# The start of the expert stage: expert 0 on unsplit weights, the third tile's weights loaded earlier, three tiles in another order

## The reference, cut to what matters

```python
def moe(h, w_router, router_bias, w_gate_l, w_up_l, w_down_l):   # cut
    scores = jax.nn.sigmoid((t @ w_router).astype(F32))
    ...                                        # best group, then top 2 of its experts
    gate = jnp.einsum('td,edf->tef', t, w_gate_l)
    up = jnp.einsum('td,edf->tef', t, w_up_l)
    act = jax.nn.silu(gate) * up * combine[..., None].astype(gate.dtype)
    return jnp.einsum('tef,efd->td', act, w_down_l).reshape(B, N, D)
```

## Time and profile before

| | us |
|---|---|
| median of 3 runs | 2196.75 (2194.47 to 2199.99) |
| the profiled execution | 2201.26 |
| its span | 2199.5 |
| TensorE busy | 1997.4 (91%) |
| VectorE, ScalarE, GpSimd busy | 1030.8, 849.7, 354.9 |

### The profile page before, as it was taken

The page is one execution under the profiler, slowest core; times in us unless marked ns, Lnnn a source line. Parts: engine busy times, 40 slices in busy tenths (PEclk is TensorE's granted clock), DMA queues, the critical chain, the costliest instruction groups (busy, mean ns, idle before and its releaser), DMA issues. The chain is left out here.

```text
span 2199.5 us, 30789 instructions
## 1 busy us (share of the span) xinstructions
PE 1997.4 (91%) x12535; PEld 1633.4 (74%) x12535; DVE 1030.8 (47%) x1744; ACT 849.7 (39%) x1375; POOL 354.9 (16%) x135
## 2 busy tenths in 40 slices
PE   5989879999999988999949898878999999799994
PEld 4889757678888876676638896557888887567663
DVE  3385246721111246777562852664111123677763
ACT  3443335431111234565434333655111133356553
POOL 2322100012213211000033222000313230200003
PEclk9999889999999998999979998999999999799997
DMA  8212686742221128999542121001212212799864
GB/s 295 72 39 79 211 287 222 259 129 73 70 74 58 44 110 325 318 309 312 194 154 74 39 78 51 1 1 39 86 58 75 70 44 96 289 401 387 302 217 172
DMA packets 163856, 336.31 MB, mean 153 GB/s; under 512 B 10370, under 2 KB 121602, under 8 KB 149252
## 3 DMA queue, kind: packets, MB, share of 16 engines
q1 hardware_dynamic: 151488, 299.63, 39.4%
q0 software_dynamic: 5760, 20.97, 2.5%
q10 hardware_dynamic: 6468, 13.73, 1.7%
HBM read 334.57 MB, written 53.74 MB: 177 GB/s over the span
## 5 line engine op out<-in xcount | busy, mean ns | idle before, releaser
L642 POOL TENSOR_TENSOR wlo<-raw,whi 128x2048 fp32r<-128x2048 f32 x52 | 238.0, 4579 | 1141.1 <-ACT whi L667 1141.1
L1656 DVE TENSOR_TENSOR xw_gu_lo<-xw_gu_raw,xw_gu_hi 128x2048 fp32r<-128x2048 f32 x100 | 228.1, 2284 | 26.6 <-ACT xw_gu_hi L1442 26.6
L184 PE MATMUL psum<-h_hi,whi 128*128 128x320 f32 x896 | 216.6, 323 | 20.4 <-POOL h_lo L177 17.7
L184 PE MATMUL psum<-whi,h_hi 128*128 128x256 f32 x720 | 209.5, 291 | 0.0
L184 PE MATMUL psum<-h_lo,whi 128*128 128x320 f32 x896 | 205.1, 310 | 0.0
L184 PE MATMUL psum<-h_hi,wlo 128*128 128x320 f32 x896 | 204.7, 309 | 0.0
L184 PE MATMUL psum<-wlo,h_hi 128*128 128x256 f32 x720 | 202.9, 282 | 0.0
L184 PE MATMUL psum<-whi,h_lo 128*128 128x256 f32 x720 | 202.8, 282 | 0.0
L814 ACT ACTIVATE sig_m<-psum 128x640 f32<-128x640 f32 x48 | 33.7, 703 | 400.1 <-PE psum L184 400.1
L1442 ACT ACTIVATE xw_gu_hi<-xw_gu_raw 128x2048 fp32r<-128x2048 f32 x100 | 185.4, 1906 | 0.0
L1795 PE MATMUL psum<-xw_d_raw,act_T 128*128 128x512 f32 x400 | 180.0, 593 | 0.9 <-ACT act_T L1468 0.9
(11 more groups left out here) (281 smaller groups left out, 3549.6 us busy)
## 6 DMA issues: line engine op xcount, KB each, us to landing
xw_gu_raw<-w_e_gate SPq DMA_DIRECT2D x50, 1024.0 KB
xw_gu_raw<-w_e_up SPq DMA_DIRECT2D x50, 1024.0 KB
xw_d_raw<-w_e_down SPq DMA_DIRECT2D x50, 1024.0 KB, 9.2
raw<-w_in SPq DMA_DIRECT2D x46, 1024.0 KB, 5.4
wm_rest<-w_mod SPq DMA_DIRECT2D x40, 1024.0 KB, 5.2
y_rows<-y_sel SPq DMA_DIRECT2D x50, 512.0 KB, 9.3
h_sel<-h_rows SPq DMA_DIRECT2D x48, 512.0 KB, 7.6
h_rows<-c_zero ACTq DMA_DIRECT2D x1, 12800.0 KB, 51.6
```

The costliest lines, as they stand in the source:

```text
L184: mm = pe.matmul(dst, st, mv[q], start=start and n == 0, stop=stop and n == 2)
L642: pool.tensor_tensor(wlo[i % 2][:, :, :], raw[i % 2][:, :, :], whi[i % 2][:, :, :].bitcast(F32), ALU.subtract).then_inc(w_lo, 1)
L1656: dve.tensor_tensor(gu_lo[i % 2][:, n, :, :], gu_raw[i % 2][:, n, :, :], gu_hi[i % 2][:, n, :, :].bitcast(F32), ALU.subtract).then_inc(x_l ...
```

## The change

Expert 0's gate/up product is done in fp32 on the weights as loaded (`gu_first`, a buffer of its own at Z + 64K) and on one unsplit copy of its rows (`h_first`), so tile 0 needs no high and low parts, and all counts of these semaphores go down by one. `gu_hi[0]` and `gu_hi[1]` change places. The gate/up load of tile 0 waits for `g_pfree` instead of the last low part of w_out. The load of tile 2's gate/up moves ahead of the wait for the scatters, behind the wait for the index steps; the rows of tiles 1 and 2 are both loaded right after the scatters. VectorE waits for the scatters before the low parts of tile 1. TensorE, ScalarE and VectorE take the first three tiles in an order written out by hand, with TensorE turning tile 2's rows after tile 1's product instead of before it.

```diff
-        gu_hi = [at(f"xw_gu_hi{i}", [P, 2, KD, DE], Z + 80 * K - 16 * K * i, F32R) for i in range(2)]
+        gu_hi = [at(f"xw_gu_hi{i}", [P, 2, KD, DE], Z + 64 * K + 16 * K * i, F32R) for i in range(2)]
+        gu_first = at("xw_gu_first", [P, 2, KD, DE], Z + 64 * K)
+        h_first = at("h_T_first", [P, KD, P], 20 * K)
...                                  # SyncE
-                            if i >= 2:
-                                sp.wait_ge(x_lo[r], i - 1)
-                            load(i, r, gu_raw[i % 2][:, n, :, :], gu_ld[i % 2])
+                            if i >= 3:
+                                sp.wait_ge(x_lo[r], i - 2)
+                            load(i, r, (gu_first if i == 0 else gu_raw[i % 2])[:, n, :, :], gu_ld[i % 2])
...
-                    sp.wait_ge(w_lo, N_STREAM - ahead)
+                    sp.wait_ge(g_pfree, 24)
                     load_gate_up(0)
                     sp.wait_ge(o_full, KD)
                     load_gate_up(1)
                     load_down(0)
+                    sp.wait_ge(w_lo, N_STREAM - ahead)
+                    sp.wait_ge(gu_ld[0], 32)
+                    sp.wait_ge(r_st, IDX_STEPS)
+                    load_gate_up(2)
                     sp.wait_ge(k_s, 16 * 2 * TT)
                     load_h(1)
-                    sp.wait_ge(r_st, IDX_STEPS)
+                    load_h(2)
                     for i in range(N_TILES):
-                        if i + 2 < N_TILES:
+                        if 1 <= i < N_TILES - 2:
                             load_gate_up(i + 2)
                             load_h(i + 2)
...                                  # ScalarE
+                    def h_whole():
+                        act.wait_ge(x_th, 1)
+                        act.activation(h_first[:, :, :].rearrange("p k s -> p (k s)"), flat(1)[:, :], ACT.Copy).then_inc(x_hh, 1)
...
-                    hi(0, "g")
-                    hi(0, "u")
-                    h_high(0)
                     hi(1, "g")
                     hi(1, "u")
+                    h_whole()
                     sigmoid(0)
                     h_high(1)
-                    for i in range(1, N_TILES):
...
+                    keep_act(0)
+                    hi(2, "g")
+                    hi(2, "u")
+                    sigmoid(1)
+                    h_high(2)
+                    for i in range(2, N_TILES):
...                                  # VectorE
-                    lo(0, "g")
-                    h_low(0)
-                    lo(0, "u")
+                    dve.wait_ge(k_s, 16 * 2 * TT)
                     lo(1, "g")
                     lo(1, "u")
                     activated(0)
                     h_low(1)
-                    for i in range(1, N_TILES):
...
+                    lo(2, "g")
+                    lo(2, "u")
+                    activated(1)
+                    h_low(2)
+                    for i in range(2, N_TILES):
...                                  # TensorE
+                    def gate_up_first():
+                        pe.wait_ge(x_hh, 1)
+                        pe.wait_ge(gu_ld[0], 32)
+                        for kc in range(KD):
+                            mm = pe.matmul(psum[:, 0, :], h_first[:, kc, :], gu_first[:, :, kc, :], start=(kc == 0), stop=(kc == KD - 1))
                         mm.then_inc(x_gu, 1)
...
-                    for i in range(N_TILES):
-                        if i >= 1:
-                            turn_act(i - 1)
-                        if i == 0:
-                            gate_up(0)
-                            turn_h(1)
-                            continue
+                    gate_up_first()
+                    turn_h(1)
+                    turn_act(0)
+                    gate_up(1)
+                    turn_h(2)
+                    down(0)
+                    for i in range(2, N_TILES):
+                        turn_act(i - 1)
                         if i + 1 < N_TILES:
                             turn_h(i + 1)
                         gate_up(i)
-                        if i >= 1:
-                            down(i - 1)
+                        down(i - 1)
```

More of the change, by code:

```diff
@@ L1388, in _ @@
                     if not last:
-                        sp.wait_ge(x_lo["g"], N_TILES)
-                        sp.wait_ge(x_lo["u"], N_TILES)
+                        sp.wait_ge(x_lo["g"], N_TILES - 1)
+                        sp.wait_ge(x_lo["u"], N_TILES - 1)
                         w_in = a["w_in"][layer + 1].rearrange("(k p) n -> p k n", p=P)
@@ L1479, in _ @@
                         keep_turned(act, f)
-                    hi(0, "g")
-                    hi(0, "u")
-                    h_high(0)
                     hi(1, "g")
                     hi(1, "u")
+                    h_whole()
                     sigmoid(0)
                     h_high(1)
-                    for i in range(1, N_TILES):
-                        if i >= 2:
-                            keep_y(i - 2)
-                        if i >= 1:
-                            keep_act(i - 1)
+                    keep_act(0)
[4 more added lines that the diff above has]
+                    for i in range(2, N_TILES):
+                        keep_y(i - 2)
+                        keep_act(i - 1)
                         if i + 1 < N_TILES:
@@ L1501, in _ @@
                     if not last:
-                        act.wait_ge(x_lo["u"], N_TILES - 1)
+                        act.wait_ge(x_lo["u"], N_TILES - 2)
                         for c in range(2):
@@ L1652, in lo @@
                         n = "gu".index(r)
-                        dve.wait_ge(x_hi[r], i + 1)
+                        dve.wait_ge(x_hi[r], i)
                         if i >= 2:
@@ L1765, in turn_h @@
                         pe.wait_ge(h_ld[i % 2], 16 * ((i + 1) // 2))
-                        pe.wait_ge(x_hl, i)
+                        if i == 1:
+                            pe.wait_ge(x_hh, 1)
+                        else:
+                            pe.wait_ge(x_hl, i - 1)
                         for kc in range(KD):
@@ L1772, in gate_up @@
                         dst = psum[:, i % 2, :]
-                        pe.wait_ge(x_hl, i + 1)
+                        pe.wait_ge(x_hl, i)
                         if i >= 2:
                             pe.wait_ge(x_ac, i - 1)
-                        pe.wait_ge(x_hi["g"], i + 1)
-                        pe.wait_ge(x_hi["u"], i + 1)
+                        pe.wait_ge(x_hi["g"], i)
+                        pe.wait_ge(x_hi["u"], i)
                         for kc in range(KD):
@@ L1780, in gate_up @@
                             pe.matmul(dst, hT_lo[i % 2][:, kc, :], gu_hi[i % 2][:, :, kc, :], start=False, stop=False)
-                        pe.wait_ge(x_lo["g"], i + 1)
-                        pe.wait_ge(x_lo["u"], i + 1)
+                        pe.wait_ge(x_lo["g"], i)
+                        pe.wait_ge(x_lo["u"], i)
                         for kc in range(KD):
                             mm = pe.matmul(dst, hT_hi[i % 2][:, kc, :], gu_lo[i % 2][:, :, kc, :], start=False, stop=(kc == KD - 1))
+                        mm.then_inc(x_gu, 1)
+                    def gate_up_first():
+                        pe.wait_ge(x_hh, 1)
+                        pe.wait_ge(gu_ld[0], 32)
+                        for kc in range(KD):
+                            mm = pe.matmul(psum[:, 0, :], h_first[:, kc, :], gu_first[:, :, kc, :], start=(kc == 0), stop=(kc == KD - 1))
                         mm.then_inc(x_gu, 1)
```

## The result

The change made the kernel slower by 0.24%: 2201.89 us (2197.34 to 2208.8, 20 runs) against 2196.61 us (2192.7 to 2201.77, 20 runs), ratio 1.0024, interval 1.0016 to 1.0031, which is 3.5 to 6.8 us. A later group of five rounds on another chip gave 1.0014 (1.0000 to 1.0027). The forecast was 2192.0, range 2184 to 2199; both the sign and the range are missed.

What follows compares the result with a forecast made beforehand. TensorE was taken to fill the steady tiles, leaving only each layer's expert-stage start to move. Third products 1.3 and 3.4 us earlier summed to 4.7 us off the 2196.75 us median, giving 2192.0, range 2184 to 2199.

Steps and rivals of the forecast that it cites:

- What bounds the kernel: Expert stage: TensorE fills the steady tiles, so only the start, up to the third tile's gate/up product, can move.
- Order of the tiles: Expert stage start: tile 1's product before tile 2's turn, both h loads after the scatters; third product at T + 20.7.
- VectorE's wait costs nothing: Before tile 1's low parts: free unless rows come 2 us earlier (about 1 us); alone, scatters end at 837.6 and 1890.3.
- Third tile's weights ahead of that wait: Load issued among the scatters shares the bus at 415 GB/s; scatters end at 842.5 and 1895.3, 2.5 and 0.5 us later.
- the forecast's own sum: Both layers' starts: third product 1.3 us earlier in layer 0 and 3.4 in layer 1, together 4.7 us less.
- fp32 product is worth zero: Tile 0's first product: ends at most 0.3 us earlier, hidden because turning tile 1 waits for the scatters; taken as zero.
- A: Expert stage start: scatters go first, tile 1's rows queue behind the weight load; 9.3 us less, 2187.5; chance 0.24.
- B: Expert stage start: scatters and tile 1's rows both go through undelayed; 14.7 us less, 2182; chance 0.09.
- C: Second product: TensorE's clock stays at 1.2 GHz, 11.7 instead of 7.7 us; slower, 2200.0; chance 0.13.

Runs made afterwards that it cites:

- Order alone: Kernel before, with only the new order: tile 2's rows loaded right behind tile 1's, tile 1's product before tile 2's turn; 2194.68 us, ratio 0.9977.
- the pair: The change with tile 2's weights loaded behind the rows, with against without VectorE's wait, in the same rounds: 2192.84 and 2191.50 us.
- fp32 alone: Kernel before, with only expert 0's gate/up product done in fp32, order and loads as before, no VectorE wait; 2196.75 us, ratio 0.9982.

## Why the prediction was wrong

**What bounds the kernel: right.** Everything was decided between the first pick and the third product; the steady stretch is as full as before in every trace (in layer 0 TensorE is busy for 212.4 to 213.0 of the 213 us from 872 on), and the third product's distance from T came out at 20.6, 21.4 and 19.2 us in layer 0 and 19.6, 21.8 and 19.3 in layer 1, where 20.7 was forecast.

**Order of the tiles: right.** Third product at T + 24.5 and T + 24.7 before, T + 20.3 in the mean after. Order alone took 8.7 us off the two starts, of which 5.4 lie behind T, and measured 0.9977.

**VectorE's wait costs nothing: right** on the time, and it does free the scatter issues: 0.95 us each after 830, the last one out at 837.25 in the second trace, 14.35 us after the first pick, against 837.67 less 820.44 = 17.2 before. But it doesn't bring T forward as I had it: without the early load T is 18.9 and 17.0 with the wait against 19.3 and 17.8 without, and with the early load 24.9 and 23.6 against 24.1 and 23.0. I had given it 1 us if the rows came early; the pair shows 1.3 us or nothing.

**Third tile's weights ahead of that wait: the step that failed, in the end of the scatters, T.** Its mechanism, two queues sharing the engines with neither first, is what the DMA table shows. Its price was mis-sized. I set the end of the scatters at the bytes left over 415 GB/s, for T = 22.1 and 21.2; measured were 24.9 and 23.6 in the mean of three traces, 2.9 and 2.4 us more. Two parts add up to that, by comparing with the two traces with the wait and without the early load (means 18.9 and 17.0):

- the scatters alone end 1.7 and 0.8 us later than my 17.2 and 16.2 (837.6 and 1890.3 less the first picks). The bus's full flow does end where I had it, 17.3 to 17.5 and 16.0 to 16.2 us after the first pick; what I left out is the tail between it and T, here 0.75 to 2.0 us;
- the load costs 6.0 and 6.6 us, not 4.9 and 5.0. While it enters, the bus carries 217 to 264 GB/s at a full share. That dip can't be the whole reason: without VectorE's wait it is as deep (209 to 262 GB/s), and the load costs only 4.8 and 5.2 us. There the slower issues leave a part of the bus free for it (a share of 0.67 to 0.74 without the load, above), where with the wait the scatters alone hold it at 0.89 to 1.02.

With the load the full flow ends 23.3 to 23.4 and 22.1 to 22.3 us after the first pick, where the bytes over 415 GB/s gave 21.8 and 20.7, and the tail is 1.0 to 2.0 us, where I had taken 0.3 and 0.5 for the receipt. What makes the tail was not found. The 16 to 25 GB/s of the one before layer 1's T are about a sixteenth of 415, so by that estimate one of the 16 engines is still at work while the others are done. It is no matter of the early load: the kernel before has the longest, and my one window over layer 1's scatters averaged over it.

The end of my range for a slow bus, 346 GB/s, was T = 24.4 and 23.3: I had it as a bound and took the other end. The load was also issued later than I had it, 3.0 us after the last index step in the first trace (832.15 against 829.15) and 2.3 in the second (833.76 against 831.44) instead of 1.9. How much of the load's price is due to that, the runs don't tell.

With the measured T the forecast's own sum becomes -4.7 + 2.9 + 2.4 = +0.6 us. The traces have no change in the mean (starts 89.2 of three, 89.3 of two before), with 6 us between the three. So the mis-sized T is 5.3 of the 10 us between forecast and measurement; for the other half see what stays open.

**fp32 product is worth zero: wrong.** I argued that the product is hidden behind the wait for the scatters, which is true, and overlooked that tile 0's two low parts on VectorE stand beside the scatters' issue. I had counted that gain under VectorE's wait. fp32 alone gives 4.1 us of the starts and measured 0.9982 (0.9971 to 0.9992); in layer 1's T the earlier issues make 0.7 us of it and the missing tail 2.2. In the change both edits free the same issues, so I take it to add little to its sum; the wait without fp32 was not run.

**The set of alternatives was too small.** I compared the change with the kernel before, not with the change less each of its parts. Asked of the early load alone, "who waits for tile 2's weights once the order is new?", the rows of before would have answered: their transfer takes 5 us and their parts some 6.5, and the product wanted them at T + 20.7. It had nothing to save and stood 2.1 MB in front of the wait that ends last. This is a loss of 8 to 9 us in time inside a change whose other parts gain 5 to 6.

**The rivals.** A and B needed T at 17.2 and 16.2; no trace of the change has that. C needed a second product of over 10.05 us; it took 8.0 and 7.1 us in the first trace, 8.15 (856.29 to 864.44) and 8.2 in the second, and 7.1 in both layers of the third. The direction that C forecast came true by another mechanism.

**What stays open.** The two starts put the change 0.6 us below the kernel before in the first pair of traces and 3.2 above it in the second; the times put it 3 to 5 above. Both traced executions of the kernel before stand above the median of their own chip, at 2201.26 against 2196.75 and 2205.99 against 2201.45 us, and no trace shows the faster half of its runs. I subtracted a difference found in one trace from a median that this trace doesn't represent. Where the typical run of the kernel before is 4.5 us faster was not found. One candidate, not shown: order alone's layer 1 has T at 17.2 instead of 20.7 with the same program ahead of T, so the kernel before may have runs with that T as well. The stretches before the first pick vary by up to 7 us between single traces of all these kernels.

## To carry to other kernels

Before moving a load ahead of a wait, ask who is late without it, in the order that the new kernel will have. If the wait is for transfers of another queue, what is put ahead of it lengthens it, here by 4.8 to 6.6 us for 2.1 MB, which take 5.1 at the full rate. And when operations are removed from an engine, look at what they stood beside as well as at what waited for them. The end of a group of transfers is not its bytes over the rate: look for a tail.

## What the runs showed of the hardware

- A 2.1 MB weight load on SyncE's queue among ten 512 KB scatters on GpSimd's delays the last scatter by 6.0 and 6.6 us when the scatters are issued without VectorE beside them (the first half costs 3.7 and 4.1, the second 2.3 and 2.5), and by 4.8 and 5.2 us when VectorE stands beside some of the issues. Both queues are served (46.1% and 39.7% of the engines). The rate falls to 209 to 264 GB/s for some 2 us as the load enters, with the DMA share at 0.87 to 1.09.
- An indirect DMA of 128 rows is issued by GpSimd in 0.95 us, beside a large VectorE operation of two SBUF inputs in 1.90 to 2.80 us.
- Ten scatters on one queue can end with a tail. In layer 1 of both traces of the kernel before, the bus's full flow ends 2.75 us before all ten have landed, and in between it carries 16 to 25 GB/s. With fp32 alone, order alone and in five of the six traces of the changed kernels without VectorE's wait the full flow ends 0.5 us before, in both layers. What makes the tail isn't settled.
- In five of the seven traces of kernels with VectorE's wait, the hand-over of the picked tile to ScalarE came 3.5 to 5.2 us after the last pick, and in several of the others up to 2.6 us after it in layer 1. In each of these traces, and in no other, many records of the scatters' landings are missing (in the first trace of the change 109 and 100 of 160 are there). In the five traces with all 160, the hand-over took 0.03 to 0.05 us. The cause isn't settled; the profile itself may be it. In the change T is the same with it and without (25.1 and 25.4). With tile 0 still split it isn't: order alone's T of 17.2 in layer 1 goes with a hand-over that is 2.6 us late.
